# Stick-breaking attention: suffix sums as two fp32r matmuls instead of one fp32 matmul

## The reference

```
z        = q k^T * scale                       # per head, 512 x 512
mask     = key_pos < query_pos
log_keep = where(mask, log_sigmoid(-z), 0)     # = -softplus(z)
suffix   = cumsum of log_keep from the right - log_keep
a        = where(mask, exp(log_sigmoid(z) + suffix), 0)
out      = a @ v
```

## Time and profile before

| | |
|---|---|
| median of 3 runs | 2182.94 us (2179.64 to 2185.81) |
| profiled execution | 2184.8 us |
| its span | 2183.0 us |
| mean granted clock of TensorE | 0.899 of 2.4 GHz |
| busy: TensorE, its weight loads | 81%, 54% of the span |
| busy: VectorE, ScalarE, GpSimd | 34%, 23%, 10% |
| HBM over the span | 170 GB/s |

### The profile page before, as it was taken

The page is one execution under the profiler, slowest core; times in us unless marked ns, Lnnn a source line. Parts: engine busy times, 40 slices in busy tenths (PEclk is TensorE's granted clock), DMA queues, the critical chain, the costliest instruction groups (busy, mean ns, idle before and its releaser), DMA issues. The chain is left out here.

```text
span 2183.0 us, 21640 instructions
## 1 busy us (share of the span) xinstructions
PE 1770.9 (81%) x8022; PEld 1177.9 (54%) x8023; DVE 752.2 (34%) x1334; ACT 499.3 (23%) x827; POOL 228.5 (10%) x265
## 2 busy tenths in 40 slices
PE   4979998887877899799959993678468899988881
PEld 3768876654343778688848881466323333333330
DVE  6334225421545677223341116643331111111114
ACT  3212334432002222222222224242011111111111
POOL 4010001000102122100030000102010001000002
PEclk9999998888988899999979985899579999999995
DMA  9312210003451775222213310015449966999983
GB/s 284 103 58 79 96 39 1 0 0 137 147 197 39 268 249 186 88 77 96 96 39 97 97 39 1 1 39 195 193 194 426 386 251 266 403 427 425 426 351 128
DMA packets 99669, 361.52 MB, mean 166 GB/s; under 512 B 21239, under 2 KB 23459, under 8 KB 87275
## 3 DMA queue, kind: packets, MB, share of 16 engines
q1 hardware_dynamic: 90791, 344.48, 41.5%
q0 software_dynamic: 5760, 9.02, 1.2%
q10 hardware_dynamic: 3012, 6.59, 0.8%
HBM read 357.28 MB, written 14.75 MB: 170 GB/s over the span
## 5 line engine op out<-in xcount | busy, mean ns | idle before, releaser
L2288 PE MATMUL x_upa<-x_ring,x_Ta 128*64 128x512 f32 x608 | 136.7, 603 | 3.3 <-DMA x_ring<-in_w_expert_up_dram 3.3
L2288 PE MATMUL x_gpa<-x_ring,x_Ta 128*64 128x512 f32 x608 | 135.2, 597 | 3.0 <-issue 1.6
L2288 PEld LDWEIGHTS x_upa<-x_ring,x_Ta 128*64 128x64 f32 x608 | 44.4, 139 | 92.7 <-issue 92.7
L2288 PEld LDWEIGHTS x_gpa<-x_ring,x_Ta 128*64 128x64 f32 x608 | 43.9, 138 | 91.0 <-issue 91.0
L317 DVE TENSOR_TENSOR p_lo<-p_raw,p_hi 128x2048 fp32r<-128x2048 f32 x18 | 41.3, 2292 | 143.2 <-ACT p_hi L670 143.2
L324 PE MATMUL fr_p<-p_hi,u_high 128*128 128x512 f32 x224 | 89.1, 398 | 0.0
L326 PE MATMUL fr_p<-p_hi,u_low 128*128 128x512 f32 x224 | 88.0, 393 | 0.0
L325 PE MATMUL fr_p<-p_lo,u_high 128*128 128x512 f32 x224 | 88.0, 393 | 0.0
L2309 PE MATMUL x_y0a<-x_ring,x_aTa 128*64 128x512 f32 x304 | 80.5, 677 | 1.2 <-ACT x_aTa L2349 1.2
L2272 PE MATMUL x_t0a<-ident,x_ga 128*128 128x128 f32 x80 | 18.5, 370 | 73.4 <-DMA x_ga<-normed_rows,x_idsa 73.4
L2309 PE MATMUL x_y1a<-x_ring,x_aTa 128*64 128x512 f32 x304 | 68.4, 592 | 0.0
(11 more groups left out here) (1010 smaller groups left out, 3986.3 us busy)
## 6 DMA issues: line engine op xcount, KB each, us to landing
x_ring<-in_w_expert_gate_dram SPq DMA_DIRECT2D x32, 2048.0 KB, 24.0
x_ring<-in_w_expert_up_dram SPq DMA_DIRECT2D x32, 2048.0 KB, 19.6
x_ring<-in_w_expert_down_dram SPq DMA_DIRECT2D x32, 2048.0 KB, 22.4
p_raw<-in_w_in_dram SPq DMA_DIRECT2D x18, 1024.0 KB, 5.1
adaw0m<-in_w_ada_dram SPq DMA_DIRECT2D x6, 2048.0 KB, 10.3
adaw1m<-in_w_ada_dram SPq DMA_DIRECT2D x6, 2048.0 KB, 9.7
fr_ada<-in_ada_w_dram SPq DMA_DIRECT2D x4, 2048.0 KB, 17.0
w_raw0m<-in_mlp_w_dram SPq DMA_DIRECT2D x8, 1024.0 KB, 6.6
```

Of the source, the lines that this page charges most:

```text
L2288: mm = nc.tensor.matmul(ps[CAP * f:CAP * f + CAP, :], self.xT[:, k, CAP * f:CAP * f + CAP], w[m + f][:, k, :], start=(k == 0), stop=(k == ...
```

## The change

The sums' matmuls get fp32r operands. `soft` is split: ScalarE copies it, rounded to fp32r, into a new tile `soft_high` (768 columns, then 512), and VectorE puts soft - soft_high, also fp32r, over the bytes of `soft` under the name `soft_low`. `tri_neg` and `ones_neg` are now fp32r tiles; their entries 0 and -1 are exact in it. Each of the ten matmuls of a head becomes two, one with the high and one with the low part. The order becomes:

```diff
-                for m, v in (..., (C.ones_neg, -1.0), (C.allow, 0.0)):
+                for m, v in (..., (C.allow, 0.0)):
...
-                dve.wait_ge(made, 13)
+                dve.wait_ge(made, 12)
                 v.tensor_copy(C.ident_r[:, :], C.ident[:, :])
                 v.tensor_scalar(C.tri_neg[:, :], C.later[:, :], -1.0, None, ALU.add)
+                v.tensor_scalar(C.ones_neg[:, :], C.ones[:, :], -1.0, None, ALU.mult)
...
-                pe.wait_ge(made, 11)
+                pe.wait_ge(made, 10)
...
+        soft_high = [s.sb(f"soft_high{i}", [P, OFF[NT]], F32R) for i in range(2)]
+        soft_low = [s.twin(f"soft_low{i}", f"soft{i}", [P, OFF[NT]]) for i in range(2)]
...
                 def sums(n):
                     half = n % 2
-                    pe.wait_ge(plus_ready, 3 * n + 2)
+                    pe.wait_ge(low_ready, 2 * n + 1)
                     for b in (3, 2, 1, 0):
                         if b == 0:
-                            pe.wait_ge(plus_ready, 3 * n + 3)
+                            pe.wait_ge(low_ready, 2 * n + 2)
                         bank, col = z[half][KEY_BANK[b]], KEY_COL[b]
                         for a in range(b, NT):
                             first = col + P * (a - b)
-                            mm = nc.tensor.matmul(bank[:, first:first + TOK - P * a],
-                                                  (C.tri_neg if a == b else C.ones_neg)[:, :], block_of(soft[half], a),
-                                                  start=False, stop=(a == NT - 1), skip_group_check=True)
+                            for part in (soft_high, soft_low):
+                                mm = nc.tensor.matmul(bank[:, first:first + TOK - P * a],
+                                                      (C.tri_neg if a == b else C.ones_neg)[:, :], block_of(part[half], a),
+                                                      start=False, stop=(a == NT - 1 and part is soft_low), skip_group_check=True)
...
+                def lows(n):
+                    half = n % 2
+                    for part, (lo, hi) in enumerate(((512, OFF[NT]), (0, 512))):
+                        dve.wait_ge(high_ready, 2 * n + part + 1)
+                        low(nc.vector, soft_low[half][:, lo:hi], soft[half][:, lo:hi], soft_high[half][:, lo:hi]).then_inc(low_ready, 1)
...
                     plus(n)
+                    lows(n)
                     plus(n + 1)
+                    lows(n + 1)
...
+                def highs(n):
+                    half = n % 2
+                    for part, (lo, hi) in enumerate(((512, OFF[NT]), (0, 512))):
+                        act.wait_ge(plus_ready, 3 * n + 2 + part)
+                        if n >= 2:
+                            act.wait_ge(exponent_ready, 2 * (n - 1))
+                        nc.scalar.activation(soft_high[half][:, lo:hi], soft[half][:, lo:hi], ACT.Copy).then_inc(high_ready, 1)
...
                     logs(n)
                     logs(n + 1)
+                    highs(n)
+                    highs(n + 1)
                     weights(n)
                     weights(n + 1)
...
-        C.tri_neg = s.sb("tri_neg", [P, P])
-        C.ones_neg = s.sb("ones_neg", [P, P])
+        C.tri_neg = s.sb("tri_neg", [P, P], F32R)
+        C.ones_neg = s.sb("ones_neg", [P, P], F32R)
```

More of the change, by code:

```diff
@@ L585, in _ @@
                 for m, v in ((C.neghalf, -0.5), (C.ident, 0.0), (C.ones, 1.0), (C.later, 0.0), (C.flip, 0.0), (C.ban, 0.0),
-                             (C.ones_neg, -1.0), (C.allow, 0.0)):
+                             (C.allow, 0.0)):
                     ch.link(pool.memset(m[:, :], v))
@@ L1379, in stick_breaking @@
         plus_ready = s.sem("sb_plus")
+        high_ready = s.sem("sb_high")
+        low_ready = s.sem("sb_low")
         exponent_ready = s.sem("sb_exponent")
```

## The result

The changed kernel takes **2188.13 us**, median of 11 runs (2183.67 to 2190.63); the kernel before takes 2182.94 in the same number of runs beside it. The ratio is 1.002, with a 95% interval of 1.0012 to 1.0027: a loss of 0.2%, small but outside what the comparison leaves uncertain.

The account below looks back on a forecast made before the run. TensorE was taken to lead, with a VectorE chain of 3.2 us before each pair. Per pair +2.6 us of stall and -2.7 of sums make -0.1, for four pairs -0.4: 2182.5 us, range 2175 to 2195.

Parts of the forecast that it names:

- Single records and their prices: Stick-breaking sums: each fp32r matmul is one record, 20 a head; a head takes 2.8 us instead of 4.54 at full clock.
- the row of bans: fp32r bans of 128 columns, 0.11 us each in the trace, taken as the price of the sums' 128-column records.
- The even head's sums 2.6 us later: Start of a pair: high and low parts delay the first sum from 485.65 to 488.25; stall 3.0 to 5.6 us.
- no wait shows between the heads: Odd head's sums behind the even head's: wait covered at half clock; at full clock 0.75 us would be seen.
- The clock: Behind a pair's first sum: half clock for 3.8 to 6.1 us, 4.9 taken; a pair's sums 7.85 us for 10.55.
- The rival in which the clock does not come back: Half clock through both heads' sums and the first weighing: +4.5 us a pair, 2201 in all; chance 0.10.
- The stage: Four pairs of stick-breaking heads: +2.6 - 2.7 = -0.1 us per pair, -0.4 in all.
- The sum: Whole program: the stage's -0.4 us taken over, setup costing nothing, 2182.5 us on the scale of the median.
- All four: -0.4 us: Stick-breaking stage: -0.1 us for each of four pairs; bounds -2.4 to +3.4.
- the rivals: Clock not back, 2201 (0.10); split hidden, 2172 (0.05); short records cheaper, 2178 (0.06); fp32 price kept, 2230 (0.01).

Follow-up runs that it names:

- the filled stalls: Unused fp32 matmuls in each stall between pairs, six in the changed kernel, three in the kernel before: 2181.75 us (0.9998) and 2179.35 us (0.9978).
- the first pair of profiles: First profile of the kernel before and of the changed one, spans 2183.0 and 2187.1 us; second profiles, both kernels unedited, 2183.2 and 2182.4.
- the eight profiles with the packet: Of the study's twenty profiles, those with an instruction packet within 1 us of VectorE's first head-norming instruction, both of the changed kernel among them; gap 0.73 to 0.92 us.
- moving one pass behind another: Kernel before, VectorE taking the odd head's absolute values behind the even head's additions instead of ahead of them: 2166.93 us (0.9915).
- the changed kernel reordered: Changed kernel, odd head's absolute values behind the even head's additions, high parts straight behind their own logarithms: 2174.98 us (0.9956).

## Why the prediction was right or wrong

- **Single records and their prices: right in sum.** Still 20 records a head. At full clock most take 0.17 us (384 columns) and 0.12 (256), as taken, though the first behind narrower ones takes 0.23 and 0.17, and a head 2.8 us. One size was off: those of 128 columns come in turns of 0.06 and 0.11 us, not 0.11 each. From TensorE's timeline of the changed kernel (start, length):

```profile
493.64 0.28 PE L1422 MATMUL stick_z<-soft_low,tri_neg 128*128 128x128 f32 x1
493.75 0.33 PE L1422 MATMUL stick_z<-soft_high,tri_neg 128*128 128x256 f32 x1
493.92 0.28 PE L1422 MATMUL stick_z<-soft_low,tri_neg 128*128 128x256 f32 x1
494.04 0.22 PE L1422 MATMUL stick_z<-soft_high,ones_neg 128*128 128x128 f32 x1
494.10 0.27 PE L1422 MATMUL stick_z<-soft_low,ones_neg 128*128 128x128 f32 x1
494.21 0.39 PE L1422 MATMUL stick_z<-soft_high,tri_neg 128*128 128x384 f32 x1
494.44 0.34 PE L1422 MATMUL stick_z<-soft_low,tri_neg 128*128 128x384 f32 x1
...
495.02 0.45 PE L1422 MATMUL stick_z<-soft_high,tri_neg 128*128 128x512 f32 x1
495.30 0.40 PE L1422 MATMUL stick_z<-soft_low,tri_neg 128*128 128x512 f32 x1
495.54 0.34 PE L1422 MATMUL stick_z<-soft_high,ones_neg 128*128 128x384 f32 x1
```

  Two of 128 take 0.17, or 0.085 each. So for 128 columns the row of bans misled, and near to it are the 81 ns of the Trainium skill, page "TensorE: Matmul & The Clock Gate", section "Back-to-back issue gap". Its 131 ns for 512 columns this trace does not show: the two here take 0.28 and 0.24. These, 0.26 on the mean where 0.224 was taken, and the slower first ones of 384 and 256 gave back what the short ones saved. So that the head came out at 2.8 is in part luck.
- **The even head's sums 2.6 us later: right.** 440.05 for a forecast of 440.1, and a stall of 5.55 us for 5.6. That no wait shows between the heads was right too.
- **The clock: right.** Half clock lasted 4.8 to 5.5 us behind a pair's first sum, for 4.9 taken; the sums of a pair 8.0 us for 7.85. The rival in which the clock does not come back did not happen. That the stall is what costs it, the filled stalls showed.
- **The stage: right within a microsecond.** +0.5 us in the first pair of profiles and -0.1 in the second, for -0.4.
- **The sum: wrong.** The step that failed is "All four: -0.4 us", taken over as the whole program's. It priced the added instructions by their durations and their handovers, inside the stage alone, and let all that follows stand at nothing, without naming a cover for it. What follows cost +3 to +5 us, on the scale of the medians, and it goes with the number of instructions ahead, so with where the later code comes to stand: the same number with nothing to do brought the loss into the kernel before (1.0015), and 16 more on each engine took it out of the changed one (0.9989). Of the rivals none had a place behind the stage.
- **What it priced well but did not use:** the prediction traced the stall to VectorE's order, and could have said that this order was worth more (17 us) than anything in the change.

What stays open is how 0.3 us at one change of blocks and 0.5 us at one wait become 3 to 5. Single profiles overlap: behind the stage one profile of the changed kernel has 1663.1 us and the other 1657.9, for 1659.1 in the first of the kernel before, and the same matmuls fall on other stretches of half clock from one execution to the next. On the mean of the twenty it can be seen. From VectorE's first copy behind the stage to its last instruction, the eight profiles with the packet take 3.3 us more than the twelve without (95% interval 1.6 to 4.9). On the time scale of the kernel before, 0.3 of it stands by 1283 us, 2.0 by 1412, 2.9 by 1516 and 3.3 by 1626, each uncertain by more than 1 us. So most of the loss builds up between 1283 and 1626 us, but what each part of it waits for was not taken apart, and no run moved these packets without moving VectorE's code.

## What to carry to other kernels

When a change trades an engine's work for a chain of waits, count the chain from the engine that stands still, and add what the clock loses behind the longer stall: here 11 us less of TensorE's work bought nothing. Look first at the order in which the helper engines take two interleaved items; moving one pass behind another gave 17 us, and the split on top of it would have cost 3 to 8 of them. Before explaining a difference of 0.2% by the changed stage, run a control that adds the same number of instructions with nothing to do, and one with twice as many.

## What had not been expected of the hardware

Instructions are loaded during the run: the page of the changed kernel, its third part, counts them over the span.

```profile
q8 instruction: 69, 1.13, 0.2%
q14 instruction: 37, 0.30, 0.0%
```

How many instructions an engine has had changes the time of code far behind them, and not in one direction. In the kernel before, 16 instructions of one column on each of two idle engines cost 3 to 4 us (2188.00), and 32 on each nothing that can be seen (2184.15). In the changed kernel, which has 16 and 17 more of its own, 16 on each took its loss away (2187.4 to 2188.1, then 2183.04), and so in the changed kernel reordered (2174.98, then 2170.34).

Behind a wait of 12 us, the first eight mixing matmuls took 6.73 us in the kernel before and 5.28 in the changed one, at the same code; other executions and kernels gave 5.1 to 6.7. How soon the clock comes back behind a stall is not a constant.
